# One encoder layer with a routed MoE on one core: the last token tile's normalisation, its transposes and its router logits are reordered, and a two-word gather is issued early

## The chip, the core and the metric

The kernel runs on one core of a Trainium2 chip. A core has five engines that run their own instruction streams and meet at semaphores: TensorE (PE) for matmuls, VectorE (DVE), ScalarE (ACT), GpSimd (POOL), and SyncE (SP), which here issues most of the DMAs. The metric is the device time of one execution in microseconds (us).

## The reference

Two groups of tokens (256 and 512, so 768 tokens or six tiles of 128) go through one encoder layer with shared weights, all in float32. The parts that matter here:

```
h  = layer_norm(x);  m = layer_norm(mem)
h  = layer_norm(a*h + mixer(h), ln1)          # attention and convolution
h  = layer_norm(a*h + cross_attention(h, m), ln2_g, ln2_b)
# MoE, on t = h:
g_logits = t @ w_rg + b_rg                    # 4 groups, the best one is taken
e_logits = t @ w_re[group] + b_re[group]      # 8 experts in it, the best two are taken
y  = sum over the two of  weight * down(silu(gate(t)) * up(t))
out = layer_norm(a*h + y, ln3)
```

A layer norm is (x - mean) * rstd * g + b for each token. The router has 36 columns in all (4 groups and 32 experts), so its logits for a tile are 128x36.

## The kernel before, in words

The program is written out by hand as five streams, one for each engine. In each, work is done in program order, and helpers put in the waits: `claim` and `was_read` wait until a bank of PSUM has been read, `full` until it has been filled. What an engine does first is therefore what stands first in its stream.

The stretch at issue lies between cross-attention and the experts. Its order is this.

- Cross-attention. The query product (`cq_term`, a seven-product scheme whose parts DVE adds up in `cq_sum`) ends with its term P3. Then PE forms scores for 24 units, each a 128x256 block (L2081), DVE takes the row maximum (`softmax`, L1418), ACT the exponential, DVE the reciprocal of the sum, POOL scales the probabilities (L851), PE turns them (L2090) and multiplies with the values (L2109). PE forms the scores of four units before it turns the first one (S_AHEAD = 3).
- Output product and second layer norm (ln2). PE runs the products (`co_term`, L2340, and `product`, L2006). As tiles get done, DVE adds the residual and takes mean and variance, POOL computes rstd (`pool_coef`, L718 to L720), and the rows are normalised. Tiles 0 to 4 share this work among ACT, POOL and DVE. The last tile, n in SHORT, is done by DVE alone (`dve_bias`): first (row - mean) * g (L754), then times rstd plus b (L757).
- Router. For each tile PE turns the normalised rows in two halves of four 128x128 blocks (`rows_T`, L2018), ACT copies both halves out of PSUM (L1002), and PE multiplies with the router's weights (`route`, L2330: eight matmuls of 128x36, each of which the trace shows as two). PE's stream ends with: turn tile 4, route 3, route 4, turn tile 5, route 5. Then DVE adds the router's bias to all six tiles' logits at once (L1756).
- Dispatch. From the logits DVE works out the two experts of each token, and with PE their ranks within the experts (L1772 to L1862). This gives index tables. POOL then gathers the rows of the first block of tokens from DRAM by an indirect DMA (`gather(0)`, index L888, DMA L905), and PE turns them (`block_T`, L2447) as the first step of the experts.
- SP's stream. As each tile is normalised, SP stores it to DRAM (L649), since the gathers read it from there. After the last one it issues weight loads of 1 MB each (L627, L632). ACT, when all six stores have landed, scales the residual rows (L1221).

POOL's stream has the routing constants (iotas, memsets) ahead of the coefficients of ln2 (`norms(LN_2)`), and the gathers behind it. `tab` is a buffer of 128x386 words that serves late in the program; at the start it holds the pattern that SP stores into a table in DRAM (semaphore `table_init`).

Of the kernel before, what the change touches and what calls it, by code (L numbers as in the profile page):

```python
# [17 lines left out]
F32 = mybir.dt.float32  # L18
# [7 lines left out]
P = 128  # L26
D = 1024
KC = D // P
# [217 lines left out]
def encoder(nc, x, mem, w_slabs, lnp, ln_cols, rope_cos, rope_sin, q_gain, k_gain, cpar_dram, w_router, b_router,  # L246
# [7 lines left out]
    with ExitStack() as ctx:  # L254
# [121 lines left out]
        lncol = sb("lncol", [P, 4, KC])  # L376
# [18 lines left out]
        tinit = tab[:, 0:T * NE // P * 2]  # L395
        gidx = [sb(f"gidx{n}", [P, 1], U32) for n in range(2)]
# [69 lines left out]
        lncol_in, resid_done = sem("lncol_in"), sem("resid_done")  # L466
        dve_step, pool_step = sem("dve_step"), sem("pool_step")
# [282 lines left out]
        def dve_bias(dve, n, link):  # L750
            rows, g, b = ln_rows(n)
            gb_wait(dve, n)
            if n in SHORT:
                link(nc.vector.scalar_tensor_tensor(out=rows, in0=rows, scalar=mv[:, n % 2, 0:1], in1=g,  # L754
                                                    op0=ALU.subtract, op1=ALU.mult))
                dve.wait_ge(ln_coef, n + 1)
                nc.vector.scalar_tensor_tensor(out=rows, in0=rows, scalar=lnc[:, n % 2, 0:1], in1=b,  # L757
                                               op0=ALU.mult, op1=ALU.add).then_inc(ln_done, 1)
                return
# [5 lines left out]
        def _(pool):  # L765
# [111 lines left out]

            norms(LN_2, lag=0)

# [109 lines left out]
        def _(act):  # L989
# [7 lines left out]
            def rows_T(layer, i):  # L997
                for j in range(2):
# [267 lines left out]
        def _(dve):  # L1266
# [405 lines left out]
            for c in range(CQ_CHUNKS):  # L1672
                was_read(dve, ("cq", "P5", c))
                cq_sum("P3", cq_out(0, 1, c), cq_out(0, 1, c), c).then_inc(free(("cq", "P3", c)), 1)
            softmax("x", CROSS, STEPS)
# [66 lines left out]
            for k in range(2 * CO_PAIRS, NT):  # L1742
# [6 lines left out]
                if k == 4:  # L1749
# [6 lines left out]
            v.tensor_tensor(lg, bank[:, 0:NT * NR].rearrange("p (t n) -> p t n", t=NT),  # L1756
                            br.rearrange("p (a n) -> p a n", a=1).to_broadcast([P, NT, NR]),
                            ALU.add).then_inc(free("route"), 1)
# [227 lines left out]
        def _(pe):  # L1986
# [22 lines left out]
            def rows_T(layer, i, rows, n):  # L2009
                if n in FOLD:  # L2010
                    pe.wait_ge(ln_hat, hats(n))
                else:
                    pe.wait_ge(ln_done, dones(n))
# [311 lines left out]
            def route(i):  # L2325

                for j in range(2):
                    was_read(pe, ("hT", 2, i, j))
                for k in range(KC):
                    last = t.matmul(logits[:, i * NR:(i + 1) * NR], catv[:, k, i * P:(i + 1) * P], wr[:, k, :],  # L2330
# [4 lines left out]
            logits = claim("route")  # L2335
            def co_term(a, term, rows, w):
# [255 lines left out]
```

## Time and profile before

| | |
|---|---|
| median of 3 runs | 1035.78 us (1035.64 to 1036.3) |
| the profiled execution | 1041.34 us, its span 1039.6 us |
| PE busy | 914.8 us (88% of the span) |
| DVE busy | 524.3 us (50%) |
| ACT, POOL busy | 237.1 us (23%), 321.1 us (31%) |
| granted TensorE clock, mean | 0.949 of full speed |

The profiled execution is one run with the profiler on. Its span runs from the first to the last instruction, and all stamps below are us from the start of that span. "Idle before" in a row of the timeline is how long the engine had nothing to run, and the arrow names what ended it. A row without it followed straight on the one before. A busy share of the whole span says little here: the work passes through stages with different limits, so the rows are read stage by stage.

### The profile page before, as it was taken

Reading aid. Unit: us, or ns where it says so; the run is one execution under the profiler, and the core shown is the slowest. Engines: PE = TensorE matmul, PEld = TensorE weight load, DVE = VectorE, ACT = ScalarE, POOL = GpSimd, SP = SyncE. Lnnn points to the kernel's source line nnn. Section 1 sums busy time; section 2 is a strip of 40 time slices with the busy share of each in tenths; the row PEclk is TensorE's granted clock in tenths of the full one; section 3 lists DMA queues with packets and bytes.
Section 4 is the critical chain, followed back from the end, with each engine's and each line's share of the span. In section 5 each row is a group of like instructions: output and inputs, shape, how many; then the busy total and the mean of one; then the engine's idle time right before and its main releaser. Section 6 shows DMA issues by size and latency. Waiting matters only on the chain.

```text
span 1039.6 us, 10109 instructions
## 1 busy us (share of the span) xinstructions
PE 914.8 (88%) x3322; PEld 472.8 (45%) x3322; DVE 524.3 (50%) x830; ACT 237.1 (23%) x582; POOL 321.1 (31%) x352
## 2 busy tenths in 40 slices
PE   4999999799989879999999999967969999999900
PEld 4555466344544434445558544553434444444300
DVE  4899999964632286746225465354311111211156
ACT  5321423234493111201004302131101111111101
POOL 6921043334453252400004403313251221112047
PEclk9999999899999999999999999977989999999955
DMA  9310301403003002220032031356997999998462
GB/s 335 135 41 0 122 0 63 100 1 82 1 1 122 1 0 81 81 82 0 1 116 88 3 160 69 154 240 223 419 404 273 420 421 418 390 416 344 182 245 121
DMA packets 46197, 165.11 MB, mean 159 GB/s; under 512 B 8640, under 2 KB 14144, under 8 KB 33856
## 3 DMA queue, kind: packets, MB, share of 16 engines
q1 hardware_dynamic: 39424, 151.85, 37.9%
q0 software_dynamic: 6720, 12.60, 3.2%
q8 instruction: 28, 0.46, 0.2%
q14 instruction: 25, 0.20, 0.1%
HBM read 156.88 MB, written 18.03 MB: 168 GB/s over the span
## 4 chain that ended last, share of the span: by engine, by line
PE 55%; POOL 4%; DVE 4%; issue 3%; DMA 2%; ACT 1%; POOLq 0%; DVEq 0%
PE ps L2470 8%; PE ps L2499 7%; PE ps L2301 7%; PE ps L2473 5%; PE ps L2340 5%; PE ps L2274 5%; PE ps L2238 4%; PE ps L2006 3%; PE ps L2184 2%; PE ps L2447 2%; PE ps L2109 2%; POOL hres L729 2%; PE ps L2081 1%; PE ps L2330 1%; PE ps L2018 1%
## 5 line engine op out<-in xcount | busy, mean ns | idle before, releaser
L1324 DVE SCALAR_TENSOR_TENSOR cat<-early,cpar,cat 128x798 f32<-128x798 f32 (+2 forms) x150 | 141.6, 944 | 4.9
L844 POOL TENSOR_SCALAR hT<-hT,rinv 128x512 f32<-128x512 f32 (+1 forms) x48 | 67.8, 1424 | 94.1 <-DVE rinv L1446 94.1
L2006 PE MATMUL ps<-ring,hT 128*128 128x512 f32 (+1 forms) x256 | 90.4, 513 | 0.0
L2006 PE MATMUL ps<-hT,ring 128*128 128x256 f32 (+1 forms) x256 | 86.1, 500 | 4.6 <-issue 2.9
L910 POOL DMA_INDIRECT pair_rows<-hT,sidx x22 | 22.1, 1002 | 182.8 <-DVE hT L1933 181.9
L1923 DVE COPY memx<-ps 128x256 f32<-128x256 f32 x22 | 9.3, 424 | 131.2 <-PE ps L2482 131.2
L2006 PEld LDWEIGHTS ps<-hT,ring 128*128 128x128 f32 x256 | 50.5, 199 | 38.8 <-issue 32.9
L718 POOL TENSOR_SCALAR lnt<-mv 128x1 f32<-128x1 f32 x28 | 14.2, 505 | 168.5 <-DVE mv L746 167.4
L2006 PEld LDWEIGHTS ps<-ring,hT 128*128 128x128 f32 x256 | 48.4, 191 | 38.7 <-issue 36.3
L1438 DVE TENSOR_REDUCE nmax<-ps 128x2 f32<-128x1024 f32 (+1 forms) x24 | 25.1, 1046 | 73.5 <-PE ps L2134 73.4
L851 POOL TENSOR_SCALAR memx<-memx,rinv 128x256 f32<-128x256 f32 x24 | 22.0, 924 | 129.7 <-DVE rinv L1402 129.7
L2499 PE MATMUL ps<-ring,memx 128*64 128x512 f32 (+1 forms) x144 | 60.0, 612 | 0.7 <-DVE memx L1923 0.7
L1933 DVE COPY hT<-ps 128x512 f32<-128x512 f32 x22 | 15.2, 692 | 67.2 <-PE ps L2499 67.2
L736 ACT ACTIVATE hres<-hres,lnc 128x1024 f32<-128x1024 f32 x22 | 27.2, 1240 | 81.8 <-POOL lnc L720 81.8
L1130 ACT ACTIVATE hT<-ps,nmax 128x512 f32<-128x512 f32 (+1 forms) x48 | 29.1, 611 | 69.6 <-DVE nmax L1438 69.5
L2470 PE MATMUL ps<-early,hT 128*64 128x512 f32 x128 | 44.0, 621 | 0.8 <-ACT hT L1230 0.8
L2473 PE MATMUL ps<-early,hT 128*128 128x512 f32 x96 | 42.5, 596 | 0.0
L2470 PE MATMUL ps<-ring,hT 128*64 128x512 f32 x96 | 42.3, 594 | 0.0
L2301 PE MATMUL ps<-hT,ring 128*128 128x384 f32 x128 | 41.6, 486 | 0.0
L1237 ACT ACTIVATE memx<-ps 128x256 f32<-128x256 f32 x22 | 8.4, 383 | 142.1 <-PE ps L2470 78.4
L1653 DVE SCALAR_TENSOR_TENSOR cat<-ps,cat 128x384 f32<-128x384 f32 x28 | 15.2, 556 | 41.2 <-PE ps L2301 41.2
L2470 PE MATMUL ps<-scr,hT 128*64 128x512 f32 x80 | 35.3, 594 | 0.8 <-ACT hT L1230 0.8
(337 smaller groups left out, 1760.6 us busy)
## 6 DMA issues: line engine op xcount, KB each, us to landing
ring<-w_down SPq DMA_DIRECT2D x16, 1024.0 KB, 17.0
early<-w_gate SPq DMA_DIRECT2D x12, 1024.0 KB, 9.5
early<-w_up SPq DMA_DIRECT2D x12, 1024.0 KB, 13.7
ring<-w_gate SPq DMA_DIRECT2D x10, 1024.0 KB, 12.3
ring<-w_up SPq DMA_DIRECT2D x10, 1024.0 KB, 16.4
scr<-w_down SPq DMA_DIRECT2D x8, 1024.0 KB, 15.6
cat<-w_down SPq DMA_DIRECT2D x8, 1024.0 KB, 15.4
scr<-w_gate SPq DMA_DIRECT2D x5, 1024.0 KB, 9.3
```

What stands on the lines that cost most here:

```text
L736: nc.scalar.activation(rows, rows, ACT.Identity, bias=lnc[:, n % 2, 1:2], scale=lnc[:, n % 2, 0:1]).then_inc(ln_hat, 1)
L844: g.tensor_scalar(sprob[u % 4][:, 0:width], sprob[u % 4][:, 0:width], rinv[:, u % 4:u % 4 + 1], None, ALU.mult).then_inc(prob_ready, 1)
L1130: a.activation(sprob[u % 4][:, 0:width], ps[:, place[key][0], 0:width], ACT.Exp, bias=nmax[:, u % 4:u % 4 + 1], accum_out=rsum[:, u % 4:u ...
L1324: ins = v.scalar_tensor_tensor(out=out, in0=src, scalar=cpar[:, c, k:k + 1], in1=out, op0=ALU.mult, op1=ALU.add)
L2006: last = t.matmul(out_of(bank), lhs(k), rhs(k), start=(k == 0), stop=(k == KC - 1))
L2238: last = t.matmul(bank, rows[:, k, :], wk[:, k, :], start=(k == 0), stop=(k == 3))
L2274: last = t.matmul(bank, rows[:, k, i * P:(i + 1) * P], wk[:, k, :], start=(k == 0), stop=(k == 3))
L2301: last = t.matmul(bank[:, 0:TH], wk[:, k, c * P:(c + 1) * P], rows[:, k, :], start=(k == 0), stop=(k == 3))
L2340: last = t.matmul(bank, rows[:, k, :], wk[:, k, :], start=(k == 0), stop=(k == 3))
L2470: last = t.matmul(gu_out(64 * h, 64 * h + 64, b), xT[b][:, k, 64 * h:64 * h + 64], gu_of(n % GU_SLOTS, k), start=(k == 0), stop=(k == KC - 1))
L2473: last = t.matmul(gu_out(0, P, b), xT[b][:, k, :], gu_of(EXPERT_BLOCKS[j][1] % GU_SLOTS, k), start=(k == 0), stop=(k == KC - 1))
L2499: last = t.matmul(ps[h0:h1, 2 + n, :], hidT[b][:, k, h0:h1], w[:, k, n * 512:(n + 1) * 512], start=(k == 0), stop=(k == 1))
```

## The change

The last tile (tile 5) is handled in another way.

- DVE still computes (row - mean) * g first, but now signals `centred` there, and PE turns these centred rows instead of the finished ones. The factor rstd and the bias b are applied to the logits: logits = rstd * (centred @ w) + (b @ w + b_router).
- The vector b @ w is prepared earlier. DVE multiplies the router's weights by a column form of b (eight tensor_scalar of 128x36, stored in `tab`), adds them up over the eight pieces (`wbsum`), and PE sums over partitions with one matmul of ones, written beside the logits. DVE's part stands ahead of the cross-attention `softmax`, PE's ahead of the output product.
- The two halves of the last tile's transposes are copied by ACT and DVE, one each, and `route` now waits for the second half only before its fifth matmul (for all six tiles).
- DVE's copy stands between the two passes of the last tile's norm, so the pass that finishes the rows comes behind it.
- The bias is added in three steps instead of one.
- POOL issues a small indirect gather of two words per partition into a spare piece of `tab`, ahead of `norms(LN_2)`.

```diff
-        lncol = sb("lncol", [P, 4, KC])
+        lncol = sb("lncol", [P, 5, KC])
...
+        wbias = tab[:, 0:KC * NR].bitcast(F32).rearrange("p (k r) -> p k r", k=KC)
+        wbsum = tab[:, KC * NR:(KC + 1) * NR].bitcast(F32)
+        spare = tab[:, (KC + 1) * NR:(KC + 1) * NR + 2]
+        first_gidx = sb("first_gidx", [P, 1], U32)
...
 # dve_bias
-                link(nc.vector.scalar_tensor_tensor(out=rows, in0=rows, scalar=mv[:, n % 2, 0:1], in1=g,
-                                                    op0=ALU.subtract, op1=ALU.mult))
+                centre = nc.vector.scalar_tensor_tensor(out=rows, in0=rows, scalar=mv[:, n % 2, 0:1], in1=g,
+                                                        op0=ALU.subtract, op1=ALU.mult)
+                if n == LN_2[-1]:
+                    centre.then_inc(centred, 1)
+                    key = ("hT", 2, NT - 1, 1)
+                    bank = full(dve, key)
+                    nc.vector.tensor_copy(catv[:, 4:8, (NT - 1) * P:T],
+                                          bank.rearrange("p (k t) -> p k t", k=4)).then_inc(free(key), 1)
+                else:
+                    link(centre)
                 dve.wait_ge(ln_coef, n + 1)
...
 # POOL
+            g.memset(first_gidx[:, :], 0).then_inc(index_zero, 1)
+            pool.wait_ge(index_zero, 1)
+            pool.wait_ge(table_init, 16)
+            g.indirect_dma_start(spare, None, table_dram, bass.IndirectOffsetOnAxis(ap=first_gidx[:, :], axis=0),
+                                 bounds_check=T * NE - 1, oob_is_err=False).then_inc(warmed, 16)
+
             norms(LN_2, lag=0)
+            pool.wait_ge(warmed, 16)
...
 # ACT, rows_T
-                for j in range(2):
+                for j in range(1 if layer == 2 and i == NT - 1 else 2):
...
 # DVE, ahead of softmax("x", CROSS, STEPS)
+            dve.wait_ge(table_init, 16)
+            dve.wait_ge(small_in, 32)
+            for k in range(KC):
+                last = v.tensor_scalar(wbias[:, k, :], wr[:, k, :], lncol[:, 4, k:k + 1], None, ALU.mult)
+            link(last)
+            v.tensor_reduce(wbsum, wbias.rearrange("p k r -> p r k"), AX.X, ALU.add).then_inc(bias_rows, 1)
...
 # DVE, the logits
-            v.tensor_tensor(lg, bank[:, 0:NT * NR].rearrange("p (t n) -> p t n", t=NT),
-                            br.rearrange("p (a n) -> p a n", a=1).to_broadcast([P, NT, NR]),
-                            ALU.add).then_inc(free("route"), 1)
+            link(v.tensor_tensor(wbsum, bank[:, NT * NR:(NT + 1) * NR], br, ALU.add))
+            v.tensor_tensor(lg[:, 0:NT - 1, :], bank[:, 0:(NT - 1) * NR].rearrange("p (t n) -> p t n", t=NT - 1),
+                            br.rearrange("p (a n) -> p a n", a=1).to_broadcast([P, NT - 1, NR]), ALU.add)
+            v.scalar_tensor_tensor(out=lg[:, NT - 1, :], in0=bank[:, (NT - 1) * NR:NT * NR],
+                                   scalar=lnc[:, LN_2[-1] % 2, 0:1], in1=wbsum, op0=ALU.mult,
+                                   op1=ALU.add).then_inc(free("route"), 1)
...
 # PE, rows_T
+                elif n == LN_2[-1]:
+                    pe.wait_ge(centred, 1)
...
 # PE, route
-                for j in range(2):
-                    was_read(pe, ("hT", 2, i, j))
                 for k in range(KC):
+                    if k % 4 == 0:
+                        was_read(pe, ("hT", 2, i, k // 4))
...
+            pe.wait_ge(bias_rows, 1)
+            t.matmul(logits[:, NT * NR:(NT + 1) * NR], ones[:, :], wbsum, start=True, stop=True)
```

What stands in the streams, at three places. First DVE at the border of the query product and cross-attention; `cat<-ps,cat` is the last part of `cq_sum`, `nmax` the row maximum. Before:

```order
L1653 SCALAR_TENSOR_TENSOR cat<-ps,cat 128x384 [waits bank_full2,bank_free2]
L1653 SCALAR_TENSOR_TENSOR cat<-ps,cat 128x384 [waits bank_full3,bank_free3]
L1418 TENSOR_REDUCE nmax<-ps 128x1 [waits bank_full0]
L1418 TENSOR_REDUCE nmax<-ps 128x1 [waits bank_full1]
L1402 RECIPROCAL rinv<-rsum 128x1 [waits bank_free0]
```

And changed:

```order
L1673 SCALAR_TENSOR_TENSOR cat<-ps,cat 128x384 [waits bank_full2,bank_free2]
L1673 SCALAR_TENSOR_TENSOR cat<-ps,cat 128x384 [waits bank_full3,bank_free3]
L1698 TENSOR_SCALAR tab<-wr,lncol 128x36 [waits small_in,table_init]
L1698 TENSOR_SCALAR tab<-wr,lncol 128x36 x7
L1700 TENSOR_REDUCE tab<-tab 128x36 [waits dve_step]
L1438 TENSOR_REDUCE nmax<-ps 128x1 [waits bank_full0]
L1438 TENSOR_REDUCE nmax<-ps 128x1 [waits bank_full1]
L1422 RECIPROCAL rinv<-rsum 128x1 [waits bank_free0]
```

Nine instructions now stand between the last sum and the first maximum. Next PE at the last tile; `hres` are the tile's rows, `cat` their transposes, `wr` the router's weights. Before:

```order
L2018 MATMUL ps<-ident,hres 128x128 [waits bank_free4,ln_done]
L2018 MATMUL ps<-ident,hres 128x128 x3
L2018 MATMUL ps<-ident,hres 128x128 [waits bank_free5]
L2018 MATMUL ps<-ident,hres 128x128 x3
L2330 MATMUL ps<-wr,cat 128x36 [waits bank_free5,bank_free4]
L2330 MATMUL ps<-wr,cat 128x36 x7
L2384 MATMUL ps<-ring,before_h 128x192 [waits bank_free2,route_dve]
```

And changed:

```order
L2049 MATMUL ps<-ident,hres 128x128 [waits bank_free4,centred]
L2049 MATMUL ps<-ident,hres 128x128 x3
L2049 MATMUL ps<-ident,hres 128x128 [waits bank_free5]
L2049 MATMUL ps<-ident,hres 128x128 x3
L2361 MATMUL ps<-wr,cat 128x36 [waits bank_free4]
L2361 MATMUL ps<-wr,cat 128x36 x3
L2361 MATMUL ps<-wr,cat 128x36 [waits bank_free5]
L2361 MATMUL ps<-wr,cat 128x36 x3
L2417 MATMUL ps<-ring,before_h 128x192 [waits bank_free2,route_dve]
```

The transposes keep their place and wait for another signal, and the eight router matmuls wait in two steps. Last DVE at the same tile, from the statistics to the first step of the choice of experts. Before:

```order
L746 BN_AGGR mv<-stats 128x2 [waits dve_step]
L754 SCALAR_TENSOR_TENSOR hres<-hres,mv,gb 128x1024 [waits gb_in,ln_stats]
L757 SCALAR_TENSOR_TENSOR hres<-hres,lnc,gb 128x1024 [waits ln_coef,dve_step]
L1756 TENSOR_TENSOR ring<-ps,br 128x216 [waits bank_full6,small_in]
L1772 TENSOR_REDUCE ring<-ring 128x6 [waits route_const,bank_free6]
```

And changed:

```order
L751 BN_AGGR mv<-stats 128x2 [waits dve_step]
L759 SCALAR_TENSOR_TENSOR hres<-hres,mv,gb 128x1024 [waits gb_in,ln_stats]
L765 COPY cat<-ps 128x4x128 [waits bank_full5]
L770 SCALAR_TENSOR_TENSOR hres<-hres,lnc,gb 128x1024 [waits ln_coef]
L1782 TENSOR_TENSOR tab<-ps,br 128x36 [waits bank_full6,small_in]
L1783 TENSOR_TENSOR ring<-ps,br 128x180 [waits dve_step]
L1785 SCALAR_TENSOR_TENSOR ring<-ps,lnc,tab 128x36
L1801 TENSOR_REDUCE ring<-ring 128x6 [waits route_const,bank_free6]
```

The copy has come in ahead of the second pass, and one bias instruction has become three.

## Rows read from the trace of the kernel before

**Rows 1.** The head of the page.

```profile
span 1039.6 us, 10109 instructions
```

**Rows 2.** The chain that ended last: start, us, engine and line; output product.

```profile
597.16 38.01 PE ps L2340 x88
```

**Rows 3.** Timeline at the start of cross-attention: start, us, engine, line, count [idle before].

```profile
546.45 3.62 PE L2081 MATMUL ps<-scr,cat 128*128 128x256 f32 x16
546.72 0.56 DVE L1653 SCALAR_TENSOR_TENSOR cat<-ps,cat 128x384 f32<-128x384 f32 x1 [2.02 <-PE ps L2301]
547.51 0.42 DVE L1418 TENSOR_REDUCE nmax<-ps 128x1 f32<-128x256 f32 x1 [0.24 <-PE ps L2081]
...
548.97 2.76 POOL L851 TENSOR_SCALAR memx<-memx,rinv 128x256 f32<-128x256 f32 x3 [111.13 <-DVE rinv L1402]
...
550.06 0.41 PE L2090 MATMUL ps<-ident,memx 128*128 128x128 f32 x2
```

**Rows 4.** Timeline of DVE, two small operations of the dispatch, for their prices.

```profile
692.73 0.49 DVE L1783 TENSOR_REDUCE ring<-ring 128x48 f32<-128x192 f32 x1
...
703.40 0.23 DVE L1847 TENSOR_SCALAR ring<-ring,gb 32x32 f32<-32x32 f32 x1
```

**Rows 5.** Timeline of the last tile, from its norm to the bias.

```profile
679.85 1.87 PE L2330 MATMUL ps<-wr,cat 128*128 128x36 f32 x16
...
682.46 3.66 PE L2330 MATMUL ps<-wr,cat 128*128 128x36 f32 x32
...
684.38 1.29 DVE L757 SCALAR_TENSOR_TENSOR hres<-hres,lnc,gb 128x1024 f32<-128x1024 f32 x1 [1.21 <-POOL lnc L720]
685.70 0.32 SPq L649 DMA_DIRECT2D h_rows<-hres  x1
...
685.95 1.07 PE L2018 MATMUL ps<-ident,hres 128*128 128x128 f32 x8
...
686.62 1.08 ACT L1002 ACTIVATE cat<-ps 128x512 f32<-128x512 f32 x2 [3.31 <-PE ps L2018]
...
687.85 2.79 PE L2330 MATMUL ps<-wr,cat 128*128 128x36 f32 x16 [0.83 <-ACT cat L1002]
...
690.75 0.38 DVE L1756 TENSOR_TENSOR ring<-ps,br 128x216 f32<-128x216 f32 x1 [5.08 <-PE ps L2330]
```

**Rows 6.** Stretches: us, busy PE, PEld, DVE, ACT, POOL; PEclk, DMA, GB/s.

```profile
180.00:183.00 3.00, 1.23 (x10) 0.82 (x10) 2.93 (x3) 2.34 (x10) 2.41 (x2) 1.00 1.05 401
183.00:187.00 4.00, 4.00 (x9) 1.61 (x8) 3.90 (x10) 0.95 (x1) 1.18 (x2) 0.57 1.04 186
688.00:689.00 1.00, 1.00 (x10) 1.00 (x10) 0.00 (x0) 0.33 (x1) 0.00 (x0) 0.87 0.99 287
705.00:706.00 1.00, 0.67 (x5) 0.57 (x6) 1.00 (x2) 0.00 (x0) 1.00 (x1) 0.50 0.64 262
872.00:873.00 1.00, 0.00 (x0) 0.00 (x0) 0.66 (x1) 0.56 (x1) 0.00 (x0) 1.00 1.09 451
```

**Rows 7.** Timeline of the first two gathers and the first turn of gathered rows.

```profile
703.51 0.19 POOL L888 TENSOR_TENSOR gidx<-tabs 128x1 uint32<-128x1 uint32 x1 [4.00 <-issue]
...
704.63 3.12 POOL L905 DMA_INDIRECT hT<-h_rows,gidx  x1 [0.93 <-POOL gidx L888]
704.77 1.81 DVE L1813 TENSOR_TENSOR hT<-ktab,ring 128x768 bf16<-128x768 f32 x2
...
707.70 1.82 DVE L1813 TENSOR_TENSOR hT<-ktab,ring 128x768 bf16<-128x768 f32 x2
707.80 0.90 POOL L888 TENSOR_TENSOR gidx<-tabs 128x1 uint32<-128x1 uint32 x1
...
710.06 1.97 PE L2447 MATMUL ps<-ident,hT 128*128 128x128 f32 x8
```

**Rows 8.** Line L905, first two gathers: ns min/median/max; then the first alone, to landing.

```profile
L905 POOL DMA_INDIRECT hT<-h_rows,gidx x2: 1002/2064/3125, 704.6 to 709.5; - x2
...
DMA to landing us min/median/max: 5.4/5.4/5.4
```

More of the change, by code:

```diff
@@ L466, in encoder @@
         lncol_in, resid_done = sem("lncol_in"), sem("resid_done")
+        centred, bias_rows, index_zero, warmed = sem("centred"), sem("bias_rows"), sem("index_zero"), sem("warmed")
         dve_step, pool_step = sem("dve_step"), sem("pool_step")
@@ L2568 @@
                          a["ln3_g"][0], a["ln3_b"][0], a["ln_mem_g"], a["ln_mem_b"]]),
-        "ln_cols": np.stack([a[n].reshape(KC, P).T for n in ("ln_in_g", "ln_in_b", "ln_mem_g", "ln_mem_b")], 1),
+        "ln_cols": np.stack([a[n].reshape(KC, P).T for n in ("ln_in_g", "ln_in_b", "ln_mem_g", "ln_mem_b")]
+                            + [a["ln2_b"][0].reshape(KC, P).T], 1),
         "rope_cos": cos, "rope_sin": sin, "q_gain": a["q_norm_g"][0], "k_gain": a["k_norm_g"][0],
```

## The prediction

> **What bounds the kernel here.** I read the chain that ended last first: from the start of the output product it is PE and nothing else [rows 2], so until the last tile a microsecond counts only if it is a microsecond of PE. Then I read the timeline at the places that the change touches.
>
> At the last tile the first edit looks at a wait that does not exist. PE runs route 3 and route 4 without a pause from 682.46, 3.66 us, and the transposes of tile 5 follow at 685.95 with no idle time before them. The finished rows were there at 684.38 + 1.29 = 685.67. PE is the late one, not the rows [rows 5]. The only gap is the one behind the transposes: 0.83 us until both copies of ACT are out, 687.85. From there on PE and DVE hand each other the work until the first turn of gathered rows at 710.06.
>
> At the border to cross-attention the reader should see a chain without slack. DVE's last sum ends at 546.72 + 0.56 = 547.28, and it then idles 0.24 us for the first scores. PE has four units of scores to run, 546.45 to 550.06, and goes straight to the first turn. That turn needs the first scaled probabilities from POOL, whose three operations take 2.76 us from 548.97, so 0.92 each: the first ends at 549.89, and 0.17 us later PE starts [rows 3]. The first maximum on DVE may not come later at all.
>
> **The change, part by part.**
>
> *Ahead of cross-attention, DVE.* Nine instructions go between the last sum and the first maximum. The price of a small tensor_scalar with a scalar per partition is 0.23 us [rows 4]. Eight behind one another, none waiting for the other, can overlap; no row shows by how much, and I take two thirds, 0.16 each: 8 x 0.16 = 1.3. The reduction handles 288 elements where the row has 192 in 0.49 us: 0.49 x 288/192 = 0.74, I take 0.6, because part of that price is fixed. Sum 1.9 us, less the 0.24 us that DVE idled: the first maximum comes 1.65 us later, and with it exponential, reciprocal, POOL and the first turn. Queued behind it on DVE is the whole softmax, and who waits is PE. From then on PE has no pause in which to catch up, for the later units start from its own scores. Cost +1.65. Bounds: with 0.10 per small one and 0.49 for the reduction, 1.3 - 0.24 = +1.05; with 0.23 and 0.74, 2.58 - 0.24 = +2.35.
>
> *Ahead of the output product, PE.* One matmul of 128x36 is two recorded ones; sixteen took 1.87 us, so +0.23 [rows 5]. PE is full from there on, nothing hides it. Bounds 0 (it fits into the wait before) and +0.4 (the two at the half clock).
>
> *The signal `centred`.* Nothing, by the first paragraph: PE reaches the transposes no earlier. Bound from below: none to gain, since nothing on PE's stream got shorter.
>
> *Two copies on two engines, the wait in two steps.* ACT's two copies take 1.08 us from 686.62 [rows 5], so the first is out half of that earlier, at 687.16, and the router matmuls start about 0.5 us earlier; DVE's copy of the second half begins when those four transposes end and is done before the fifth matmul comes up. On top there is the clock. Sixteen recorded matmuls took 1.87 us for tile 2 and 2.79 us for tile 5, because the granted clock fell to half within 688 to 689 (mean 0.87) [rows 5, 6]. If it falls at the same distance from the transposes, half a us more of the matmuls runs at full speed. I take -0.75. Bounds: 0 (it falls half a us earlier too) and -0.5 - 0.92 = -1.4 (it stays up).
>
> *The bias in three steps.* One instruction of 0.38 becomes 128x36, a wait for it, 128x180 and 128x36. With 0.23 for each small one, 0.33 for the middle, and 0.1 of overlap: 0.69 - 0.38 = +0.3; bounds +0.1 and +0.45. All of it stands behind PE's last matmul and ahead of the whole choice of experts, so it counts.
>
> *The finished rows come later.* The second pass of the norm moves from 684.38 behind DVE's copy, which ends near 687.8. It ends at about 689.1 instead of 685.67: 3.4 us later. Behind `ln_done` SP holds the store of tile 5 and then the weight loads; behind the store wait ACT's scaling and POOL's first gather. The store and the scaling have time: the gather's index is only ready at 703.51 [rows 7]. The loads are needed by later blocks. But they keep the DMA engines full until within 705 to 706 (share 0.64 there) [rows 6]; moved by 3.4 us they end near 709. The first gather, issued at 704.63, landed 5.4 us later, at 710.0 [rows 7, 8], in an otherwise idle DMA. PE, which was not seen to wait for it, starts at 710.06. So there is no slack: gather and loads now run side by side. If the gather moved nothing before the loads end and then takes as long as it did, it lands 1.2 us late; if its packets go in between, not late at all. I take +0.3 (bounds 0 and +1.2).
>
> *The early gather on POOL.* The issue itself costs nothing: POOL has only constants around it, and the first coefficients of ln2 come much later. What it could give is 2.1 us: the first real gather held POOL 3.12 us, the second 1.00 [rows 7, 8]. But PE reaches the first turn through its own chain with DVE (the second and third L1813, then its matmuls) without a recorded wait, so a gather that lands at 708 changes nothing by itself. I take 0 for it; it can only pay for the lateness of the loads. Bounds -0.05 and 0 (the rival below lets it count).
>
> The 3.12 us may not be a first-time price at all. The row says what lay beside it: DVE's L1813 from 704.77 to 706.58. The index copy at 707.80, beside the next L1813 at 707.70, took 0.90 where the same copy took 0.19 [rows 7]. The Trainium skill, page "SBUF — State Buffer", section "Who interferes with whom", states that a DVE instruction with two SBUF inputs and a GpSimd instruction that reads SBUF exclude each other, and that the loser waits for the whole instruction. This trace agrees in these two rows. By that rule the early gather shortens nothing, the real one would still take about 3.1 us, and the term for gather and loads would be the upper +1.2 rather than +0.3.
>
> Sum: 1.65 + 0.23 - 0.75 + 0.3 + 0.3 = +1.73 us. The profiled execution took 1041.34 us with a span of 1039.6 [rows 1]; it would be 1043.1. The runs' median lies 5.6 us below the profiled one, and I put the same difference on it: 1035.78 + 1.73 = 1037.5.
>
> **Rivals.**
>
> *The pause also costs the clock (slower).* The 1.65 us pause comes in cross-attention between the fourth scores and the first turn. At 180 to 183 PE was busy only 1.23 of 3 us, and in the next 4 us the mean clock was 0.57. Against it: a whole us without PE work at 872 to 873 left the clock at 1.00 [rows 6]. If it falls here, as at 183, some 3.3 us of PE work run at half speed and cost 1.6 more: +3.3, 1039.1. [...]
>
> *The bias work is nearly hidden.* If the nine instructions cost at their lower bound or PE has slack that the rows don't show, the first term is under half a us: 0.4 + 0.23 - 0.75 + 0.3 - 0.1 = about 0, 1035.9. For it: DVE idles a lot over cross-attention. Against it: 0.17 us from POOL's end to PE's start is a hand-over, not slack.
>
> *The first gather was the gate (faster).* Its landing at 710.0 and PE's start at 710.06 are too close to tell which was waited for. If the turn waited for it, 2.1 us could go; with the clock held over the router (-1.4) and the bias work cheap (0.4 + 0.23 + 0.3) that is about -2.6: 1033.2. Against it, PE's own chain ends there too.
>
> *Gather and loads in each other's way.* The upper bound of that term, 1.2 in place of 0.3: +2.6, 1038.4. POOL is then held beside DVE's L1813 as before [rows 7], and the change doesn't do what its early gather is for. Against it: the loads have ended, or nearly, when the gather's rows move.
>
> **How the numbers follow.** The forecast 0.42, the fallen clock 0.20, the hidden bias work 0.20, the gate 0.10, gather and loads 0.08. About 0.2% (2.07 us) is what a measurement of this kernel can tell from no change: 1033.7 to 1037.85. The forecast sits inside, but near the edge: 0.30 inside, 0.12 above. Hidden bias work 0.18 inside, 0.02 below. The gate 0.10 below, clock and collision 0.26 above, 0.02 inside. So faster 0.12, same 0.50, slower 0.38. The forecast's own lower ends together give 1.05 - 1.4 + 0.1 = -0.25 (1035.5), its upper ends 2.35 + 0.4 + 0.45 + 1.2 = +4.4 (1040.2). The range goes from 1033.6, which leaves out most of the gate, to 1040.2, beyond the fallen clock, and leaves out under 2 in 10.
>
> **What would show it.** In the changed profile: a pause of PE near 550 ahead of its first turn in cross-attention, with DVE's reduction of `tab` ending 1.7 us after its last sum; the transposes of tile 5 right behind route 4 with no idle time; the router matmuls of tile 5 about 0.5 us behind ACT's first copy; the store of tile 5 issued 3.4 us later against the transposes; and the first gather's hold of POOL, 1.0 us (first-time price) or again 3 us (port). I am wrong if PE passes 550 without a pause, or if the turn at 710 moves by more than 1 us against the router's end.

## The result, and the profile after

The changed kernel is slower: 1043.92 us (median of 10 runs, 1041.75 to 1046.14), against 1038.36 us for the kernel before (10 runs, 1034.91 to 1043.26, the three of the base among them). The ratio is 1.0054, with a 95% interval of [1.0034, 1.0074], so about 5.6 us (3.5 to 7.7). The prediction said 1037.5, within 1033.6 to 1040.2. Of the 6.4 us that it missed, 2.6 are its base, since before's median here is above the 1035.78 it started from, and 3.8 are the change of the median, +5.6 against +1.73. Before's ten runs lie in two groups, five at 1034.91 to 1036.92 us and five at 1039.80 to 1043.26; the three of the base are all in the lower one, before's profiled execution (1041.34) lies with the upper one, and every run of the changed kernel took 1041.75 or more.

The profiled execution of the changed kernel took 1043.73 us, where the prediction had 1043.1. Its page begins so, against [rows 1]:

```profile
span 1042.0 us, 10122 instructions
```

The span is 2.4 us longer. I followed it in four places, in the order of the program. First the timeline at the start of cross-attention, which answers to [rows 3] (start, us, engine, line, operation, count, [idle before <- what ended it]):

```profile
546.74 3.62 PE L2112 MATMUL ps<-scr,cat 128*128 128x256 f32 x16
547.01 0.56 DVE L1673 SCALAR_TENSOR_TENSOR cat<-ps,cat 128x384 f32<-128x384 f32 x1 [2.02 <-PE ps L2332]
547.49 1.27 DVE L1698 TENSOR_SCALAR tab<-wr,lncol 128x36 f32<-128x36 f32 x8
548.79 0.65 DVE L1700 TENSOR_REDUCE tab<-tab 128x36 f32<-128x288 f32 x1
549.36 0.74 DVE L1438 TENSOR_REDUCE nmax<-ps 128x1 f32<-128x256 f32 x2
...
550.66 2.76 POOL L864 TENSOR_SCALAR memx<-memx,rinv 128x256 f32<-128x256 f32 x3 [112.54 <-DVE rinv L1422]
...
551.76 0.41 PE L2121 MATMUL ps<-ident,memx 128*128 128x128 f32 x2 [1.40 <-POOL memx L864]
```

The nine DVE instructions take 1.27 + 0.65 us, the first maximum comes at 549.36, and PE, which ran through at 550.06 before, now idles 1.40 us for POOL. Next the timeline of the last tile, which answers to [rows 5]:

```profile
684.37 3.66 PE L2361 MATMUL ps<-wr,cat 128*128 128x36 f32 x32
...
687.87 1.07 PE L2049 MATMUL ps<-ident,hres 128*128 128x128 f32 x8
688.53 0.60 ACT L1022 ACTIVATE cat<-ps 128x512 f32<-128x512 f32 x1 [3.31 <-PE ps L2049]
688.97 0.69 DVE L765 COPY cat<-ps 128x512 f32<-128x512 f32 x1 [4.25 <-PE ps L2049]
689.18 1.98 PE L2361 MATMUL ps<-wr,cat 128*128 128x36 f32 x16 [0.25 <-ACT cat L1022]
689.58 1.28 DVE L770 SCALAR_TENSOR_TENSOR hres<-hres,lnc,gb 128x1024 f32<-128x1024 f32 x1
690.88 0.32 SPq L654 DMA_DIRECT2D h_rows<-hres  x1
...
691.27 0.20 DVE L1782 TENSOR_TENSOR tab<-ps,br 128x36 f32<-128x36 f32 x1 [0.41 <-PE ps L2361]
691.50 0.35 DVE L1783 TENSOR_TENSOR ring<-ps,br 128x180 f32<-128x180 f32 x1
691.76 0.25 DVE L1785 SCALAR_TENSOR_TENSOR ring<-ps,lnc,tab 128x36 f32<-128x36 f32 x1
```

The transposes still follow route 4 without idle time. The router matmuls start 0.25 us behind the transposes instead of 0.83 and take 1.98 us instead of 2.79. The store, which stood 0.25 us ahead of the transposes, is issued 3.01 us behind their start. Then the stretches, which answer to [rows 6] (us, busy PE, PEld, DVE, ACT, POOL, then PEclk, DMA share, GB/s):

```profile
688.00:689.00 1.00, 0.94 (x9) 0.70 (x7) 0.03 (x1) 0.47 (x1) 0.00 (x0) 1.00 0.00 0
692.00:693.00 1.00, 0.00 (x0) 0.00 (x0) 0.83 (x6) 0.00 (x0) 0.00 (x0) 0.54 1.09 377
705.00:706.00 1.00, 0.49 (x3) 0.32 (x4) 0.91 (x4) 0.00 (x0) 0.61 (x1) 0.50 0.99 418
711.00:712.00 1.00, 0.11 (x2) 0.00 (x0) 0.49 (x3) 0.00 (x0) 0.00 (x0) 0.50 0.69 254
```

At 688 the DMA engines, at share 0.99 before, stand still, because the loads wait behind the store. In return they are full at 705 to 706, where they ran dry before (0.64), and run dry only within 711 to 712. Last the timeline of the first gather, which answers to [rows 7]:

```profile
704.39 0.19 POOL L908 TENSOR_TENSOR gidx<-tabs 128x1 uint32<-128x1 uint32 x1 [4.01 <-issue]
...
705.39 1.14 POOL L925 DMA_INDIRECT hT<-h_rows,gidx  x1 [0.81 <-POOL gidx L908]
705.64 1.81 DVE L1842 TENSOR_TENSOR hT<-ktab,ring 128x768 bf16<-128x768 f32 x2
706.56 0.94 POOL L908 TENSOR_TENSOR gidx<-tabs 128x1 uint32<-128x1 uint32 x1
...
709.67 1.44 PE L2433 MATMUL ps<-ring,hT 128*128 128x96 bf16 x12 [1.50 <-DVE hT L1842]
...
713.18 1.12 PE L2480 MATMUL ps<-ident,hT 128*128 128x128 f32 x4 [2.07 <-DMA hT<-h_rows,gidx]
```

The early gather seems to have helped: the first real one holds POOL for 1.14 us and not 3.12. Yet PE waits for its rows, 2.07 us, where before it did not wait at all. The view of line L925, the first gather alone, answers to the last line of [rows 8]:

```profile
DMA to landing us min/median/max: 7.7/7.7/7.7
```

So the landing takes 7.7 us from the start of the gather instead of 5.4, though POOL is done with the gather 2 us sooner after its start. The last of the seven loads lands just ahead of it, as the timeline of its issue and the view of the DMA issues (KB, us to landing) say: 694.96 + 18.0 = 712.96 against 705.39 + 7.7 = 713.09.

```profile
694.96 0.66 SPq L632 DMA_DIRECT2D cat<-w_up  x1
...
cat<-w_up SPq DMA_DIRECT2D x1, 1024.0 KB, 18.0
```

Putting the stretch in five pieces makes the kernels comparable whatever came earlier in an execution. Each number is the difference of two starts, read in the timeline or (the output product) in the chain of waits; the runs e1 to e11 come below.

| us from ... to ... | before | after | e11 | e1 | e5 | e2 | e4 | e9 | e10 |
|---|---|---|---|---|---|---|---|---|---|
| first scores to output product | 50.71 | 52.49 | 52.49 | 50.72 | 50.71 | 52.52 | 50.71 | 50.76 | 52.51 |
| output product to transposes of tile 5 | 88.79 | 88.64 | 88.63 | 88.79 | 88.79 | 88.62 | 88.79 | 88.79 | 88.91 |
| transposes to the bias on DVE | 4.80 | 3.40 | 3.95 | 3.40 | 4.80 | 3.41 | 3.40 | 3.41 | 5.51 |
| bias to the first gather's index | 12.76 | 13.12 | 12.77 | 13.12 | 12.76 | 13.11 | 13.12 | 12.77 | 13.12 |
| index to PE's turn of gathered rows | 6.55 | 8.79 | 6.58 | 8.93 | 9.19 | 6.52 | 6.52 | 6.62 | 7.28 |
| sum | 163.61 | 166.44 | 164.42 | 164.96 | 166.25 | 164.18 | 162.54 | 162.35 | 167.33 |

Before to after: +1.78 - 0.15 - 1.40 + 0.36 + 2.24 = +2.83 us.

### The profile page after: what moved, and what is told of

It reads as the page before. It is cut to its first block, busy times and chain, and to the rows that moved or that the text cites. A ratio compares the mean times of both kernels' runs of the same rounds, so it can differ in the third digit from the quotient of the medians.

```text
span 1042.0 us, 10122 instructions
## 1 busy us (share of the span) xinstructions
PE 918.4 (88%) x3324; PEld 472.8 (45%) x3324; DVE 526.7 (51%) x842; ACT 236.8 (23%) x581; POOL 319.7 (31%) x354
## 4 chain that ended last, share of the span: by engine, by line
PE 55%; POOL 4%; issue 3%; DVE 3%; DMA 2%; ACT 1%; POOLq 0%; SPq 0%; DVEq 0%
PE ps L2503 8%; PE ps L2532 7%; PE ps L2332 7%; PE ps L2506 5%; PE ps L2373 5%; PE ps L2305 5%; PE ps L2269 4%; PE ps L2035 3%; PE ps L2215 2%; PE ps L2480 2%; PE ps L2140 2%; POOL hres L734 2%; DMA hT<-h_rows,gidx 2%; PE ps L2112 1%; PE ps L2361 1%
## 5 line engine op out<-in xcount | busy, mean ns | idle before, releaser
L2215 PE MATMUL ps<-ring,cat 128*128 128x512 f32 x64 | 32.9, 662 | 6.4 <-DVE hres L1481 4.5
```

The source lines that it names most:

```text
L2215: last = t.matmul(bank, catv[:, k, i * P:(i + 1) * P], w[:, k, :], start=(k == 0), stop=(k == KC - 1))
```

## The experiments

Theory, after the first look: the loss is the pause in cross-attention plus a collision at the end. The late store holds back the seven weight loads behind it in SP's stream (four wait for the store alone, the other three for the router's end too), the first gather is issued into them and lands when they end. Rival for the collision: the gather itself, late for another reason (the early gather, POOL's own pace). Rival for the pause: it is made up later.

**e1_bias_after_softmax** takes the pause away from the changed kernel.

```diff
                 cq_sum("P3", cq_out(0, 1, c), ...).then_inc(free(("cq", "P3", c)), 1)
+            softmax("x", CROSS, STEPS)
             dve.wait_ge(table_init, 16)
...
             v.tensor_reduce(wbsum, ...).then_inc(bias_rows, 1)
-            softmax("x", CROSS, STEPS)
...
             logits = claim("route")
-            pe.wait_ge(bias_rows, 1)
-            t.matmul(logits[:, NT * NR:(NT + 1) * NR], ones[:, :], wbsum, start=True, stop=True)
...
             h2_T(NT - 1)
+            pe.wait_ge(bias_rows, 1)
+            t.matmul(logits[:, NT * NR:(NT + 1) * NR], ones[:, :], wbsum, start=True, stop=True)
             done("route", route(NT - 1))
```

> The changed kernel with the bias preparation elsewhere: DVE's nine instructions behind the cross-attention softmax (where DVE idles 4.5 us), PE's matmul of ones between the last transposes and the last router matmuls (where PE waits for the copies). Theory (pause): the 1.40 us wait of PE ahead of its first turn in cross-attention and the 0.23 us matmul go away, everything behind comes 1.9 us earlier, and PE's wait for the first gather (2.07 us) stays, since gather and loads move together: 1.9 us below the changed kernel, about 1042.0 against 1043.9. Rival (the loss is made in the experts' stage alone, whatever comes before): within 0.5 us of the changed kernel.

Measured: 1041.58 us (12 runs), ratio to before 1.0018 [1.0002, 1.0035]. The first piece falls back to 50.72 us, before's value, and the matmul of ones costs nothing beside the wait for the copies (3.40). The wait for the gather stays, as the timeline shows:

```profile
702.79 1.14 POOL L925 DMA_INDIRECT hT<-h_rows,gidx  x1 [0.82 <-POOL gidx L908]
...
710.72 1.97 PE L2480 MATMUL ps<-ident,hT 128*128 128x128 f32 x8 [2.21 <-DMA hT<-h_rows,gidx]
```

So in these pieces pause and collision are separate terms.

**e2_loads_first** lets four of the seven loads go ahead of the last store (the expectation counts five). They no longer wait for the finished rows at all, so they go earlier than in the kernel before.

```diff
+                if i == NT - 1:
+                    full(sp, ("co", NT - 1, 1))
+                    load_d(1, 1)
+                    load_gu(3, 3)
+                    load_d(2, 2)
                 sp.wait_ge(ln_done, dones(LN_2[i]))
                 sp.dma_start(h2_dram[i * P:(i + 1) * P, :], hres[:, i, :]).then_inc(h2_stored, 16)
-            full(sp, ("co", NT - 1, 1))
-            load_d(1, 1)
-            load_gu(3, 3)
-            load_d(2, 2)
```

> The changed kernel with one edit on SP: the five weight loads of 1 MB each that stood behind the store of the last tile (w_down 1, gate and up of expert 3, w_down 2) are issued ahead of it, so they no longer wait for the finished rows. Theory (loads collide with the first gather): the loads end several us before the first gather's rows move, the gather lands 4 to 5.5 us after its issue instead of 7.7, PE's wait of 2.07 us ahead of its first turn of gathered rows goes, and the time falls by 2 us, to about 1041.9; the pause in cross-attention stays. Rival (the gather is late for its own sake, by the indirect DMA's own latency): it still lands near 7.7 us after issue, no change in time.

Measured: 1040.78 us (12 runs), ratio 1.0008 [0.9991, 1.0025]. Timeline of the first load, the store and the same two instructions as above, then the landing from the view of the gather's line:

```profile
681.79 0.33 SPq L637 DMA_DIRECT2D ring<-w_down  x1
...
691.59 0.33 SPq L659 DMA_DIRECT2D h_rows<-hres  x1
...
706.10 1.14 POOL L926 DMA_INDIRECT hT<-h_rows,gidx  x1 [0.82 <-POOL gidx L909]
...
711.61 1.94 PE L2481 MATMUL ps<-ident,hT 128*128 128x128 f32 x8
```

```profile
DMA to landing us min/median/max: 3.4/3.4/3.4
```

The same gather, as long after its index as in the changed kernel (1.0 us), lands after 3.4 us and PE does not wait. The store is as late as there, 3.02 us behind the start of the transposes (688.57), so it is the loads that hold the gather up and not the store.

**e5_before_late_loads** makes the collision alone, in the kernel before: SP waits for the router's logits ahead of the last store.

```diff
+                if i == NT - 1:
+                    full(sp, "route")
                 sp.wait_ge(ln_done, dones(LN_2[i]))
```

> The kernel before with one edit on SP: the store of the last tile, and so the weight loads behind it, waits until the router's last matmuls are done (690.65 instead of 685.7 in the kernel before, 5 us later). Nothing else is changed. Theory (loads collide with the first gather): the loads end near 710 instead of 705.7, the first gather's rows land near 712 instead of 710, PE waits about 2 us ahead of its first turn of gathered rows, and the time rises by about 2 us. Rival (what costs in the changed kernel is only the pause in cross-attention; the gather's rows go in between the loads): no wait of PE there, no change of time.

Measured: 1042.99 us (12 runs), ratio 1.0037 [1.0017, 1.0057]. Every piece but the last is before's to 0.01 us; the last is 2.64 us longer. Timeline:

```profile
690.28 0.32 SPq L651 DMA_DIRECT2D h_rows<-hres  x1
...
704.24 3.12 POOL L907 DMA_INDIRECT hT<-h_rows,gidx  x1 [0.94 <-POOL gidx L890]
...
712.31 1.97 PE L2449 MATMUL ps<-ident,hT 128*128 128x128 f32 x8 [2.46 <-DMA hT<-h_rows,gidx]
```

With e2, which takes the collision out while the store stays late, this shows the cause: late loads, whatever the rest of the change does.

**e11_pause_alone** gives the kernel before the preparation of b @ w and the matmul of ones, its result not used.

```diff
...
+            dve.wait_ge(table_init, 16)
+            dve.wait_ge(small_in, 32)
+            for k in range(KC):
+                last = v.tensor_scalar(wbias[:, k, :], wr[:, k, :], lncol[:, 4, k:k + 1], None, ALU.mult)
+            link(last)
+            v.tensor_reduce(wbsum, wbias.rearrange("p k r -> p r k"), AX.X, ALU.add).then_inc(bias_rows, 1)
             softmax("x", CROSS, STEPS)
...
             logits = claim("route")
+            pe.wait_ge(bias_rows, 1)
+            t.matmul(logits[:, NT * NR:(NT + 1) * NR], ones[:, :], wbsum, start=True, stop=True)
...
```

> The kernel before with the preparation of b @ w alone: nine DVE operations ahead of the cross-attention softmax and the one matmul of ones ahead of the output product, its result not used; the rest of the last tile, the loads and the gathers as before. If the step of my sum holds (pause +1.65, matmul +0.23), PE's first turn of probabilities comes 1.4 to 1.9 us later against its scores than before, and the kernel takes +1.9 us (ratio about 1.0018). If the pause also costs TensorE's clock in cross-attention, +3 us or more. If cross-attention makes it up again (the hidden-work rival), within 0.5 us of before. The gather at the first turn lands as before, and PE does not wait for it.

Measured: 1042.67 us (12 runs), ratio 1.0025 [1.0006, 1.0043]. The first piece is 52.49 us, the changed kernel's value. The clock does not fall in the pause: granted 1.00 from 547 to 557, as in the changed kernel. Two things in the timeline, the pause and the last tile:

```profile
552.87 0.41 PE L2099 MATMUL ps<-ident,memx 128*128 128x128 f32 x2 [1.40 <-POOL memx L854]
...
688.97 1.07 PE L2027 MATMUL ps<-ident,hres 128*128 128x128 f32 x8
...
690.87 1.95 PE L2339 MATMUL ps<-wr,cat 128*128 128x36 f32 x16 [0.83 <-ACT cat L1005]
...
692.92 0.38 DVE L1765 TENSOR_TENSOR ring<-ps,br 128x216 f32<-128x216 f32 x1 [4.59 <-PE ps L2339]
```

The last tile is built here as in the kernel before, and still its router matmuls run at full speed: 1.95 us, where [rows 5] had 2.79. So the fallen clock there does not come with this code each time (in e5, where the last tile is built so too, it fell again: 4.80 us in the third piece), and e10 below shows the same of the changed kernel.

**e9_two_copies_alone** gives the kernel before the two copies and the wait in two steps, nothing else.

```diff
 # DVE, behind the finished rows of the last tile
+                if n == LN_2[-1]:
+                    key = ("hT", 2, NT - 1, 1)
+                    bank = full(dve, key)
+                    nc.vector.tensor_copy(catv[:, 4:8, (NT - 1) * P:T],
+                                          bank.rearrange("p (k t) -> p k t", k=4)).then_inc(free(key), 1)
...
 # ACT
-                for j in range(2):
+                for j in range(1 if layer == 2 and i == NT - 1 else 2):
...
 # PE
-                for j in range(2):
-                    was_read(pe, ("hT", 2, i, j))
                 for k in range(KC):
+                    if k % 4 == 0:
+                        was_read(pe, ("hT", 2, i, k // 4))
```

> The kernel before with one part of the change alone: the last tile's transposes (of the finished rows, as before) are copied by ACT and DVE, one half each, and the router's matmuls wait for the second half only before the fifth. No signal on the centred rows, no bias preparation, no early gather. Theory (PE reaches the transposes no earlier, so the signal on centred rows gives nothing, and all of the gain is here): the transposes follow route 4 without a pause, the router ends 1.4 us earlier against them, nothing is paid for it, and the first turn of gathered rows comes about 1.3 us earlier: 1.3 us below the kernel before. Rival (the centred rows are what lets the router end early): the router's end moves by less than 0.6 us.

Measured: 1039.09 us (12 runs; before beside it 1040.1), ratio 1.0003 [0.9984, 1.0022]. Timeline, for the last tile and the turn:

```profile
685.84 1.07 PE L2023 MATMUL ps<-ident,hres 128*128 128x128 f32 x8
...
687.16 1.98 PE L2335 MATMUL ps<-wr,cat 128*128 128x36 f32 x16 [0.25 <-ACT cat L1007]
...
708.64 1.97 PE L2452 MATMUL ps<-ident,hT 128*128 128x128 f32 x8
```

All that the changed kernel gained from the transposes to the bias (3.40 us) is here too (3.41), without `centred` and without rstd on the logits. The 1.3 us expected in time do not show: the medians lie 1.0 us apart, the recorded ratio, which is not that of the medians, says none, and half a microsecond is below what 12 runs can tell.

**e4_both** is e1 and e2 together.

> Both edits together: the bias preparation behind the softmax and the loads ahead of the last store. Theory (two separate losses that add up): 1.9 + 2.1 = 4.0 us below the changed kernel, about 1040, with PE's wait ahead of the first turn of gathered rows gone, and the first turn about 1 us earlier than in the kernel before, so 1 us below it in the profile. Rival (one hides the other): only about 2 us below the changed kernel.

Measured: 1039.03 us (12 runs), ratio 0.9993 [0.9972, 1.0014]. The two costs add up: against the changed kernel the pieces fall by 1.48 us in e1, 2.26 in e2 and 3.90 here. With both out, the five pieces sum to 162.54 us, 1.07 less than before. But 0.85 of that is the clock that had fallen in before's third piece (4.80 against 3.95 in e11), so some 0.2 us is left as the worth of the change, and the time cannot be told from before's. Neither this nor e9 is shown to beat the kernel before.

**e10_changed_again** is the changed kernel a second time.

> The changed kernel once more, for its time beside the others of this call. Theory (pause 1.7, matmul 0.25, router -1.4, bias steps 0.35, wait for the gather 2.1, all in the profile): 3 to 4 us above the kernel before. Rival (a further loss that the profile does not show): 5 us or more above.

Measured: 1042.14 us (12 runs), ratio 1.0031 [1.0013, 1.0049]. The ratio says +3.2 us (1.4 to 5.1): the theory of the expectation, 3 to 4 us, and of the interval only the very end reaches its rival's 5. In its profiled execution the clock fell ahead of the last tile. Timeline, then the stretch from 688 to 689, where the clock (the third number from the end) is at half and was at 1.00 in the first profile of this kernel:

```profile
686.33 1.95 PE L2049 MATMUL ps<-ident,hres 128*128 128x128 f32 x8
...
688.11 3.63 PE L2361 MATMUL ps<-wr,cat 128*128 128x36 f32 x16
...
688.00:689.00 1.00, 1.00 (x7) 0.90 (x5) 0.69 (x2) 0.06 (x1) 0.00 (x0) 0.50 0.00 0
```

The third piece is 5.51 us here and 3.40 in the other profile of the same code. The late index then takes part of the collision away (7.28 us in the last piece).

**e3_no_early_gather, e6_gather_held_back, e7_no_early_dve_later** ask what made the first gather short. e3 is the changed kernel without the early gather; e6 keeps it and puts two small memsets between index and gather; e7 is e3 with two small DVE copies (128x6 each) ahead of the wide operation.

```diff
 # e3
...
-            g.indirect_dma_start(spare, None, table_dram, ...).then_inc(warmed, 16)
...
 # e6, POOL
                 row_index(j, 0, gidx[j % 2], gidx_ready)
+                if j == 0:
+                    for n in (2, 3):
+                        g.memset(first_gidx[:, :], 0).then_inc(index_zero, 1)
+                        pool.wait_ge(index_zero, n)
 # e7, DVE, on top of e3
+            for _ in range(2):
+                link(v.tensor_copy(den, rankf[0]))
```

> The changed kernel without the early gather. Theory (shared port): the first real gather is held beside DVE's L1842 and not by being the first; with the early one gone it takes 3 us only if it starts as close ahead of L1842 as before (0.14 us), else about 1.3 us as the early gather itself took (1.32 us). Rival (first-time price): it takes about 3.1 us wherever it stands. For the time both say little: the loads keep the DMA full until 711.7, so the rows land at about 713 either way, within 0.5 us of the changed kernel.

> The changed kernel, its early gather kept, with two tiny memsets on POOL between the index and the first real gather, so that this gather starts some 0.3 us later, no longer ahead of DVE's L1842 but beside it. Theory (shared port): the gather is held until L1842 has ended and takes about 3 us in spite of the early gather. Rival (first-time price, which the early gather has paid): it takes 1.0 to 1.2 us as in the changed kernel.

> The changed kernel without the early gather, and with two small copies (128x32 each, linked) on DVE ahead of the second of its two wide products with the rank tables, so that DVE's wide operation starts some 0.4 us later and after the first real gather has begun on POOL. In the run without the early gather alone, POOL's gather began 0.13 us ahead of DVE's operation and took 3.12 us. First-time theory (the first indirect gather of the program costs 2 us more, whatever lies beside it): the gather takes 3.1 us again, though it begins 0.5 us or more ahead of DVE's operation. Port theory (POOL is held beside DVE's wide operation with two SBUF inputs): a gather that is done or nearly done when DVE's operation starts takes 1.0 to 1.4 us. The time of the run is not what is asked.

Measured: e3 1044.08 us (12 runs), ratio 1.0045 [1.0029, 1.0062], so the early gather changes the time of the kernel by nothing that shows. e6 (one run, 1040.61 us) decides nothing: the memsets were swallowed by a shorter gap, and the gather still started 0.20 us ahead of DVE's operation (1.14 us). The timeline of e3 and then that of e7 (one run, 1042.34 us) tell the reason of the 3.12 us:

```profile
705.98 3.12 POOL L918 DMA_INDIRECT hT<-h_rows,gidx  x1 [0.94 <-POOL gidx L901]
706.11 1.81 DVE L1835 TENSOR_TENSOR hT<-ktab,ring 128x768 bf16<-128x768 f32 x2
```

```profile
704.02 1.31 POOL L918 DMA_INDIRECT hT<-h_rows,gidx  x1 [0.94 <-POOL gidx L901]
704.20 0.41 DVE L1877 COPY gb<-ring 128x6 f32<-128x6 f32 x2
704.64 1.83 DVE L1835 TENSOR_TENSOR hT<-ktab,ring 128x768 bf16<-128x768 f32 x2
```

Both are the program's first gather. With DVE's wide operation 0.13 us behind its start it takes 3.12 us, with 0.62 us it takes 1.31. The difference, 1.81 us, is just the length of DVE's recorded operations. So it is a hold beside DVE, not a first-time price. A price of first use is left, but it is small: 1.31 against 1.14 in the instruction and a gap of 0.94 against 0.81 ahead of it. In the kernels with the early gather the first real one started 0.20 to 0.25 us ahead of DVE's operation and was not held; whether this tenth of a microsecond or the early gather itself kept it free, no run separates.

## Why the prediction was wrong, step by step

**Two steps failed. The first: gather and loads, +0.3 (bounds 0 and +1.2).** It measured +2.24 in the profile (2.07 of it PE's recorded wait), and +2.64 when made alone (e5). The prediction's own sign of being wrong came true: PE's turn moved by 2.6 us against the bias on DVE (12.76 + 6.55 against 13.12 + 8.79). The mechanism was named, the size was not, for two reasons. First, I set the end of the loads, 709, against a gather issued when it was before. But the path between transposes and index got shorter, by 1.40 - 0.36 = 1.04 us, while the store went 3.26 us the other way against the same transposes. The loads run dry some 20 us behind the store's issue in both kernels (685.70 and 705 to 706, 690.88 and 711 to 712). That was about 2 us behind the index (703.51) before and is about 7 us behind it now (704.39): the two moves add up to some 5 us, where I had counted 3.4. A gain between the store and the index deepens the collision, as a loss there relieves it (e10); a gain ahead of both leaves it as it is: e1 with its clean first piece still waits 2.21 us. Second, the +0.3 let most of the gather's rows get in between the loads. In fact the gather lands 0.1 to 0.3 us behind the last load: 713.09 against 712.96 here, 710.69 against 710.5 in e1, 712.24 against 711.9 in e5. The upper bound of +1.2 did wait for the loads (709 and then some 2.2 us, as from POOL's end to the landing before), but with their end set too early.

**The second: from the profile to the median, -5.6 us.** The prediction put the profiled execution at 1043.1 and the median 5.6 us below it, because it lay so in the kernel before. The profiled execution took 1043.73, but the median lies 0.2 us above it. That is 5.8 of the 6.4 us missed. The difference was taken from three runs at 1035.64 to 1036.3 and one profile at 1041.34; before's ten runs have their median at 1038.36. And that the profile came out within 0.7 us is luck in part: the gather's +1.9 over its term was offset by the clock and the copies (-0.65), by the pause and the matmul (-0.25) and by what lies outside the five pieces (-0.4).

**The pause, +1.65, and the matmul of ones, +0.23.** Right: 1.41 for the pause, and 1.78 - 0.15 = 1.63 us for the first two pieces together, against 1.88. It is the same in e11, where the time also says so (1.0025). The rival that the pause costs the clock is out (1.00 throughout), and so is the rival that it is hidden.

**`centred`, nothing.** Right. The transposes follow route 4 in both kernels, and e9 has the whole gain without it.

**Two copies, -0.75.** The copies were sized right, but the clock was not a property of the change. At the same full clock the third piece takes 3.95 us in e11 and 3.40 in the changed kernel: -0.55, against "about 0.5" in the working. The other 0.85 of the profile's -1.40 is the clock that had fallen in before's profiled execution [rows 6] and fell earlier still in e10. I should have left it out of the sum: it comes and goes between executions of one kernel.

**The bias in three steps, +0.3.** Right: +0.36, in every run that has it.

**The early gather, 0.** Right for the time (e3). It did shorten the first gather, 3.12 to 1.14, which I had put down to a first-time price and doubted in the next paragraph. The Trainium skill, page "SBUF — State Buffer", section "Who interferes with whom", has a two-input DVE instruction and a GpSimd instruction that reads SBUF exclude each other. e7 agrees that the 1.81 us is DVE's. What I concluded from the page, that the real gather would still take 3.1 us, did not come: it took 1.14 us, and from 705.64 to 706.53 it and DVE's operation ran side by side, DVE's two instructions taking 1.81 us as ever. With the early gather it started 0.25 us ahead of DVE's operation instead of 0.14 [rows 7]; that this was what kept it free is likely but not shown. The upper +1.2, which I tied to the page, would have been nearer to the measured +2.24, but for another reason: with the same 1.14 us on POOL the gather lands after 7.7 us behind the loads and after 3.4 without them (e2). The rival that the first gather was the gate is out too: in e2 it lands 2 us sooner after its start than before, and the turn comes 6.52 us behind the index instead of 6.55.

**What stays open.** With the clock's share put aside, the five pieces give +2.83 + 0.85 = +3.7 us: inside the measured 3.5 to 7.7 but at its lower end, and inside the 1.4 to 5.1 of the second measurement (e10). The single costs by ratio, 0.0025 and 0.0037 and 0.36 us of bias, sum to 2.6 + 3.8 + 0.36 = 6.8 us, less 0.5 for the copies. Each is uncertain by 2 us. Outside the five pieces the profiles show no further loss: the first scores come 0.29 us later than before (546.74 against 546.45), and from PE's turn to the end of the span the changed kernel takes 328.8 us against 329.5. What two profiles cannot show is the clock of the other executions. A mean granted clock above 0.950 was reached in 39 of 129 runs of the kernels whose gather does not meet the late loads (before beside the experiments, e2, e4, e9, e11), but in 3 of 58 of those where it does (the changed kernel, e10, e1, e3, e5). Of before's 29 runs beside e10 the nine at 0.952 to 0.954 took 1035.43 to 1037.42 us, the others, at 0.950 or less, 1039.37 or more. So the collision goes together with a lower clock over the whole kernel, which may hold the rest of the 5.6 us; that it is the cause is not shown.

## What to carry to other kernels

An instruction that is moved behind another takes along everything its signal releases: here one DVE pass held a store, and the store held the loads of 1 MB behind it, which then stood in front of a gather on the path. Set such a transfer's end against the new time of what it can collide with, and let every gain on the path between count against you. Read the clock's part of a stage from several executions before it is booked as a gain or a loss. And before a median is forecast from a profile, see where that profile lies among the kernel's runs.

## What the runs showed that I had not expected

- A gather issued behind a backlog of loads lands with the end of the backlog: 7.7 to 8.0 us after its start and 0.1 to 0.3 us behind the last load (the changed kernel, e1, e5), against 3.4 us without loads beside it (e2).
- Without the early gather, the first gather took 3.12 us when it started 0.13 to 0.14 us ahead of DVE's wide operation (five profiles) and 1.31 us when it started 0.62 us ahead (e7). With the early gather it took 1.14 us at 0.20 to 0.25 us ahead (six profiles).
- From the transposes to the bias, the same last tile took 3.95 us (e11) or 4.80 us (before, e5) in the old form and 3.40 or 5.51 us in the changed kernel, by when the granted clock fell from its full level to half.
